# A one-core decoder layer in f32: the up stage of its experts in two passes, with the weights as the stationary operand

## The chip, the cores and the metric

The kernel runs on one core of a Trainium2 chip. The metric is the device time of one execution in microseconds; shown are the median of three executions and one profiled execution.

## What is computed

One decoder layer on 256 tokens of width 2048: a combined input projection, two kinds of attention, gates, an output projection, a layer norm, then a retrieval over 128 x 128 = 16384 single-neuron experts, and a last layer norm. The change sits in the last two:

```python
def peer(x, w_query, sub_keys_1, sub_keys_2, expert_down, expert_up):
    ...
        u = expert_down[et]
        h = jax.nn.gelu(jnp.einsum('cd,ced->ce', xt, u), approximate=False)
        vv = expert_up[et]
        return jnp.einsum('ce,ced->cd', gt * h, vv)
...
        y_p = peer(h, peer_w_query[l], ...)
        h = layer_norm(ALPHA * h + y_p, ln2_g[l], ln2_b[l])
```

Each token picks 128 experts (8 heads, 16 each) with gates. The kernel does it densely: it multiplies all experts' down rows with the tokens, takes gelu, multiplies by a gate matrix g that is zero except at the picks, and multiplies with all up rows. Only the last 16 tokens (`ROUTED`) are left out of the dense down product (`DENSE` = 240): their picked down rows are gathered.

## The kernel before

**Weights.** All weights come as a stream of 425 tiles of 128 x 2048 f32, each in two halves of 128 x 1024 (512 KB). SP loads a half into `raw` (four slots, refilled as soon as `lo_ready` says that DVE is done with it). For full precision each half is split: ACT copies it to an fp32r high part (`hi`, L461), DVE subtracts to get the low part (`lo`, L779). PE then makes three products: high x high, high x low, low x high. Two tiles are in work at a time: ACT and DVE make tile n+1 while PE uses tile n, and a half's slot is free when PE has used it (`half_used`).

**Down stage** (`down`, 128 tiles). For each 128 experts the weights are stationary (128 x 128) and the tokens move. High and low parts of the tokens lie side by side, 480 columns, so that one pass with the high weight makes two products (L1552, L1556), and one of 240 columns with the low weight the third (L1553, L1555). ACT and DVE add the two parts and take gelu; the result `act4` goes to `a_dram` in HBM, four tiles at a time, written by ACT's queue. Beside it DVE selects the top experts, and POOL scatters the gates into `g_dram` by indirect DMAs (L396), gathers the down rows of the 16 routed tokens (L403), and adds their results into g by 16 more indirect DMAs (`put_pair`, L413).

**Up stage** (`up`, L1577, 128 tiles of 128 experts x 2048 outputs). Here the multiplied activations m = a x g are stationary (128 experts x 128 tokens, high and low part) and the weights move, 256 columns at a time: two token halves, two weight halves, three products, four chunks, 48 matmuls a tile. All 8 banks of PSUM hold the sum. POOL loads a and g for four tiles at a time (`loads`, L381 and L382, two buffers); DVE multiplies (`m_mult`, L1199), ACT makes the high part (`m_high`, L687), DVE the low (`m_low`, L1204). The last two tiles are done bank by bank with 512 columns (`up_bank`, L1587 to L1589), so that the norm can begin.

**Last norm.** Tokens are on partitions. For each of two token halves: residual from `h1_n` (h1 in token order, made by 32 transposes at L1538 and 8 copies at L683 ahead of the down stage), sum by accumulators, squares on ACT, times `ln2_g`, plus `ln2_b`, and stores of 256 KB by SP.

**What sets the order.** Nothing is scheduled: each engine runs its own program in the order written, with semaphores between them. A wait holds everything behind it on its engine.

Of the kernel before, what the change touches and what calls it, by code (L numbers as in the profile page):

```python
# [80 lines left out]
PAIR_AT = [134, 139, 144, 149, 155, 160, 165, 170]  # L81
# [17 lines left out]
N_SMALL = 4 * KD + 2 * KL + 8  # L99
# [44 lines left out]
def build(nc, stream, x_t, const_in, small_in, keys_t, ln2, rows_dram, y_out, a_dram, g_dram):  # L144
# [5 lines left out]
    def sem(name):  # L150
# [12 lines left out]
    sb("gap_a", [P, 96])  # L163
    a_all = sb("a_all", [P, KD, 2 * T], F32R)
# [25 lines left out]
    h1_n = sb("h1_n", [P, TT, D], F32, peer_mem)  # L190
    ln2_s = sb("ln2_s", [P, 2, D], F32, peer_mem)
# [11 lines left out]
    query_mem.close()  # L203
    sc = sb("sc", [P, TT, 2 * PEER_HEADS, NKEYS], F32, down_mem)
    act4 = sb("act4", [P, 2, 4, T], F32, down_mem)
    work = sb("work", [P, TOPK * TOPK], F32, down_mem)
    cand = sb("cand", [P, TOPK * TOPK], F32, down_mem)
    pick = sb("pick", [P, 2, TOPK, TOPK], F32, down_mem)
    val = sb("val", [P, 3, TOPK], F32, down_mem)
    idx = sb("idx", [P, 3, TOPK], U32, down_mem)  # L210
    idx2 = sb("idx2", [P, 2, TOPK], U32, down_mem)
    idx_f = sb("idx_f", [P, 4, TOPK], F32, down_mem)
    slot = sb("slot", [P, 2, TOPK], F32, down_mem)
    lists = sb("lists", [P, TT, 3, GROUPS, COLUMNS], U32, down_mem)
    routed = sb("routed", [P, 3, COLUMNS], U32, down_mem)
    h_rows = sb("h_rows", [P, D], F32, down_mem)
    part = sb("part", [P, 2, DENSE], F32, down_mem)
    u_b = sb("u_b", [P, COLUMNS], F32, down_mem)
    val_b = sb("val_b", [P, COLUMNS], F32, down_mem)
    down_mem.close()  # L220
    up_mem = ExitStack()

    a_in = sb("a_in", [P, 2, 4, T], F32, up_mem)
    g_in = sb("g_in", [P, 2, 4, T], F32, up_mem)
    m_f = sb("m_f", [P, 2, T], F32, up_mem)
    sb("gap_m", [P, 96], F32, up_mem)
    m_hi = sb("m_hi", [P, 2, T], F32R, up_mem)
    m_lo = sb("m_lo", [P, 2, T], F32R, up_mem)
    y_s = sb("y_s", [P, TT, D], F32, up_mem)
    u_s = sb("u_s", [P, TT, D], F32, up_mem)  # L230
    sums = sb("sums", [P, TT, 4], F32, up_mem)
    squares_s = sb("squares_s", [P, TT, 4], F32, up_mem)
    moment = sb("moment", [P, TT, 4], F32, up_mem)
    junk = sb("junk", [P, 4, 512], F32, up_mem)
    up_mem.close()
# [13 lines left out]
    x_in, par_in, keys_in, ln2_in = [sem(f"x_in{q}") for q in range(4)], sem("par_in"), sem("keys_in"), sem("ln2_in")  # L249
# [20 lines left out]
    ones_ready, rows_in, routed_in, row_in = sem("ones_ready"), sem("rows_in"), sem("routed_in"), [sem(f"row_in{b}") for b in range(ROW_BUFS)]  # L270
    part_ready, gelu_done = sem("part_ready"), sem("gelu_done")
    dot_ready, ub_gelu, vb_ready, b_put = sem("dot_ready"), sem("ub_gelu"), sem("vb_ready"), sem("b_put")
    ag_in = [sem("ag_in0"), sem("ag_in1")]
    m_ready, mhi_ready, mlo_ready, y_ready = sem("m_ready"), sem("mhi_ready"), sem("mlo_ready"), sem("y_ready")
    nmean_ready, sd_ready, out_ready, y_done = (
        sem("nmean_ready"), sem("sd_ready"), sem("out_ready"), sem("y_done"))
    dve_step, act_step = sem("dve_step"), sem("act_step")

    a_flat = a_all.rearrange("p k t -> p (k t)")
    up_hi = a_flat[:, 16:16 + 2 * HALF].rearrange("p (s n) -> p s n", s=2)  # L280
    up_lo = a_flat[:, KD * T + 16:KD * T + 16 + 2 * HALF].rearrange("p (s n) -> p s n", s=2)

    def weights(t, hf, moved=False):

        return (up_hi[:, t.par, :], up_lo[:, t.par, :]) if moved and hf else (w_hi[t.slot(hf)], w_lo[t.slot(hf)])

    row_buf = [m.rearrange("p k t -> p (k t)")[:, D * b:D * b + D] for m in (qp, res) for b in range(2)]
# [5 lines left out]
    r_sq = h1_n.rearrange("p t (q n) -> p (t q) n", q=2)  # L293
# [32 lines left out]
    def _(sp):  # L326
# [20 lines left out]
        for tt in range(TT):  # L347
            for c in range(4):
                o = slice(512 * c, 512 * c + 512)
                sp.wait_ge(out_ready, 4 * tt + c + 1)  # L350
                sp.dma_start(y_out[tt][:, o], u_s[:, tt, o]).then_inc(y_done, 16)
        sp.wait_ge(y_done, 16 * 4 * TT)
# [3 lines left out]
    def _(pool):  # L356
# [20 lines left out]
        pool.wait_ge(h1_lo, KD)  # L377
        pool.dma_start(ln2_s[:], ln2.partition_broadcast(P)).then_inc(ln2_in, 16)
# [5 lines left out]
        pool.wait_ge(ht_ready, 8)  # L384
        for j in range(GROUPS):
            pool.dma_start(h_rows[ROUTED * j:ROUTED * j + ROUTED, :], h1_n[ROUTED_AT:P, 1, :]).then_inc(rows_in, 16)
# [1307 lines left out]
```

## Time and profile before

| | us |
|---|---|
| median of 3 executions (2403.88 to 2408.3) | 2405.1 |
| the profiled execution's own time | 2408.02 |
| its span (first to last instruction) | 2406.3 |
| PE busy in the span | 2387.1 |
| up stage's matmuls in the chain (L1577) | 685.75 |

The profile is of one execution; its time stands 2.9 us above the median and 1.7 above its span. PE is busy for nearly all of the span, but a busy engine may still be slowed or replaced, and the time that counts is the chain that ended last.

### The profile page before, as it was taken

The numbers are of one execution on the slowest core, as the hardware profiler recorded it, in microseconds if no ns is written. First come the engines' busy times: TensorE is split into PE (matmuls) and PEld (weight loads), VectorE is DVE, ScalarE is ACT, GpSimd is POOL, SyncE is SP. The second block draws the span as 40 slices with busy tenths as digits, with TensorE's granted clock in tenths as the row PEclk, the third lists the DMA queues.
The fourth block names the chain that finished last, engine by engine and source line by source line (L and its number), as shares of the span: only waits on it lengthen the run. The fifth ranks groups of instructions, "written<-read, shape, count | busy, mean of one in ns | idle before, by whom it ended". The sixth has DMA issues, their size and how long they took to land.

```text
span 2406.3 us, 50917 instructions
## 1 busy us (share of the span) xinstructions
PE 2387.1 (99%) x18832; PEld 2318.2 (96%) x18832; DVE 1568.7 (65%) x2620; ACT 1198.8 (50%) x1787; POOL 592.3 (25%) x428
## 2 busy tenths in 40 slices
PE   9999999999999999999999999999999999999997
PEld 9999999999999999999999999999999999999997
DVE  5555555646666666888888887755555555555556
ACT  5444444545554444666565655444444444444444
POOL 0000000000000000477668886786000000000000
PEclk9999999999999999999999999999999999999999
DMA  7666676554445665588888889988776677777764
GB/s 275 220 216 222 216 224 207 187 192 158 162 152 175 195 197 185 189 229 223 229 257 258 261 273 288 287 232 256 250 239 237 244 244 244 233 241 244 247 232 148
DMA packets 182974, 539.26 MB, mean 224 GB/s; under 512 B 53680, under 2 KB 53680, under 8 KB 180480
## 3 DMA queue, kind: packets, MB, share of 16 engines
q1 hardware_dynamic: 124128, 449.89, 56.0%
q0 software_dynamic: 54176, 71.81, 12.1%
q10 hardware_dynamic: 4608, 16.78, 2.3%
q8 instruction: 32, 0.52, 0.1%
q14 instruction: 30, 0.25, 0.0%
HBM read 501.55 MB, written 35.78 MB: 223 GB/s over the span
## 4 chain that ended last, share of the span: by engine, by line
PE 97%; DVE 2%; ACT 1%; DMA 0%; issue 0%; ACTq 0%; SPq 0%; DVEq 0%
PE ps L1301 37%; PE ps L1577 28%; PE ps L1556 9%; PE ps L1552 9%; PE ps L1555 5%; PE ps L1553 5%; PE ps L1340 1%; PE ps L1355 1%; PE ps L1342 0%; PE ps L1348 0%; PE ps L1370 0%; DVE w_first L779 0%; PE ps L1530 0%; PE ps L1356 0%; PE ps L1335 0%; ACT w_first L461 0%
## 5 line engine op out<-in xcount | busy, mean ns | idle before, releaser
L779 DVE TENSOR_TENSOR w_first<-raw,w_first 128x1024 fp32r<-128x1024 f32 x425 | 520.6, 1225 | 379.7 <-ACT w_first L461 379.3
L396 POOL DMA_INDIRECT g_dram<-lists x256 | 438.8, 1714 | 99.2 <-issue 81.5
L461 ACT ACTIVATE w_first<-raw 128x1024 fp32r<-128x1024 f32 x425 | 447.2, 1052 | 4.0 <-DMA raw<-stream 3.1
L779 DVE TENSOR_TENSOR w_second<-raw,w_second 128x1024 fp32r<-128x1024 f32 x299 | 366.0, 1224 | 3.2 <-ACT w_second L461 3.0
L461 ACT ACTIVATE w_second<-raw 128x1024 fp32r<-128x1024 f32 x299 | 314.2, 1051 | 4.7 <-DMA raw<-stream 4.3
L1301 PE MATMUL ps<-a_all,w_first 128*128 128x256 f32 x2472 | 307.7, 280 | 0.0
L1301 PE MATMUL ps<-a_all,w_second 128*128 128x256 f32 x2472 | 300.2, 277 | 0.2 <-DVE a_all L810 0.2
L1301 PEld LDWEIGHTS ps<-a_all,w_first 128*128 128x128 f32 x2472 | 292.3, 188 | 1.0
L1301 PEld LDWEIGHTS ps<-a_all,w_second 128*128 128x128 f32 x2472 | 290.4, 188 | 0.4 <-DVE a_all L810 0.4
L1577 PE MATMUL ps<-w_first,m_hi 128*128 128x256 f32 x2016 | 269.6, 276 | 0.0
L1577 PE MATMUL ps<-a_all,m_hi 128*128 128x256 f32 x1984 | 265.2, 276 | 0.0
L779 DVE TENSOR_TENSOR a_all<-raw,a_all 128x1024 fp32r<-128x1024 f32 x126 | 154.4, 1225 | 150.4 <-ACT a_all L461 150.4
L1577 PEld LDWEIGHTS ps<-w_first,m_hi 128*128 128x128 f32 x2016 | 247.3, 188 | 0.1
L1577 PEld LDWEIGHTS ps<-a_all,m_hi 128*128 128x128 f32 x1984 | 243.2, 188 | 0.0
L461 ACT ACTIVATE a_all<-raw 128x1024 fp32r<-128x1024 f32 x126 | 133.8, 1062 | 170.7 <-PE ps L1577 170.7
L1556 PE MATMUL ps<-a_all,w_second 128*128 128x480 f32 x512 | 193.9, 379 | 0.0
L1552 PE MATMUL ps<-a_all,w_first 128*128 128x480 f32 x512 | 193.8, 379 | 0.0
L1556 PE MATMUL ps<-a_all,w_first 128*128 128x480 f32 x512 | 193.7, 378 | 0.0
L1552 PE MATMUL ps<-a_all,w_second 128*128 128x480 f32 x512 | 193.6, 378 | 0.0
L692 ACT ACTIVATE part<-ps 128x240 f32<-128x240 f32 x128 | 47.6, 372 | 285.6 <-PE ps L1556 285.6
L381 POOL DMA_DIRECT2D a_in<-a_dram x32 | 17.1, 534 | 632.7 <-DVE m_f L1199 630.6
L687 ACT ACTIVATE m_hi<-m_f 128x256 fp32r<-128x256 f32 x128 | 53.3, 417 | 206.6 <-DVE m_f L1199 206.6
(245 smaller groups left out, 4399.0 us busy)
## 6 DMA issues: line engine op xcount, KB each, us to landing
raw<-stream SPq DMA_DIRECT2D x850, 512.0 KB, 3.4
g_dram<-rot POOLq DMA_DIRECT2D x32, 512.0 KB, 6.1
a_dram<-act ACTq DMA_DIRECT2D x32, 512.0 KB, 3.7
a_in<-a_dram POOLq DMA_DIRECT2D x32, 512.0 KB, 5.1
g_in<-g_dram POOLq DMA_DIRECT2D x32, 512.0 KB, 6.4
g_dram<-lists POOLq DMA_INDIRECT x256
res<-x_t SPq DMA_DIRECT2D x4, 512.0 KB, 7.4
ln_s<-ln POOLq DMA_DIRECT2D x1, 2048.0 KB, 8.3
```

Of the source, the lines that this page charges most:

```text
L396: pool.indirect_dma_start(out=g_cell, out_offset=bass.IndirectOffsetOnAxis(ap=lists[0:n, tt, 1, j, c:c + 1], axis=0), in_=lists[0:n, tt, 2 ...
L461: act.activation(weights(t, hf, moved)[0], raw[:, t.slot(hf), :], ACT.Copy).then_inc(hi_ready, 1)
L687: act.activation(m_hi[:, par, :], m_f[:, par, :], ACT.Copy).then_inc(mhi_ready, 1)
L692: act.activation(part[:, t.par, :], acc[t.par][:, DENSE:2 * DENSE], ACT.Copy).then_inc(part_ready, 1)
L779: dve.tensor_tensor(low, raw[:, s, :], high.bitcast(F32), ALU.subtract).then_inc(lo_ready, 1)
L1301: ins = pe.matmul(out, w, a, start=first and q == 0, stop=last and q == 2)
L1340: ins = pe.matmul(ps_s[:, o:o + k1], q_s[:, q0:q0 + P], k_s[:, 0:k1], start=True, stop=not rope)
L1552: pe.matmul(both, wh, a_all[:, kk, 0:2 * DENSE], start=kk == 0, stop=False)
L1553: ins = pe.matmul(high, wl, a_all[:, kk, 0:DENSE], start=False, stop=False)
L1555: pe.matmul(high, wl, a_all[:, kk, 0:DENSE], start=False, stop=False)
L1556: ins = pe.matmul(both, wh, a_all[:, kk, 0:2 * DENSE], start=False, stop=kk == KD - 1)
L1577: ins = pe.matmul(ps[:, o:o + 256], m[:, b % 2, s], w[:, 256 * c:256 * c + 256], start=first and q == 0 and c % 2 == 0, stop=False, skip_g ...
```

## The change

**Up stage.** It now has the form of the down stage: the weights are stationary, 128 x 128, and m moves, its high and low parts side by side in `m_two` (480 columns, high weight), then 240 columns with the low weight. Outputs lie on partitions: one bank of PSUM for 128 outputs, 8 banks for 1024. So the experts are gone through twice, pass 0 for outputs 0 to 1023 and pass 1 for the rest, 64 tiles each; a tile's two halves are now two blocks of 128 experts x 1024 outputs. The stream has the same number of halves. PE makes 32 matmuls a tile.

**m in pass 1.** A block of four (512 experts, 32 of them, `BLOCKS`) is multiplied by g once in pass 0 (`m_mult`, one instruction of 960 columns, at every second tile) and stays in SBUF where there is room: 21 slots (`SLOTS_M`). The first 6 results of gelu never go to HBM (`KEPT`). Blocks 19 to 31 share two slots in pass 0, so that POOL's `load` of block u, from 21 on, waits for `mlo_ready` of block u-2. Pass 1 begins with the last two blocks, then the 19 resident ones, and loads and multiplies the last 11 again.

**Routed tokens.** g is no longer changed for them (`put_pair` is gone). Their up rows are gathered by 16 indirect DMAs of 128 rows (`x_fetch`), DVE scales and adds them (`x_add`, at every third tile of pass 1 from tile 70 on), and 16 small matmuls sum over each token's eight groups (`x_sums`, between tiles 119 and 120).

**Between the passes.** The last tile of pass 0 is done bank by bank (`by_bank`); ACT copies the low part (`low_s`), DVE adds the high part to the residual, and the first tile of pass 1 goes bank by bank too.

**Last norm.** Features are on partitions. The residual times ALPHA minus its mean is made early (`hsum`, one matmul, `scale_res`). At the end the sum over features and squares is made by matmuls with ones; DVE centres and scales 16 x 256 columns, ACT applies gain and bias, and SP stores `y_out` as features x tokens. 16 transposes and 4 copies ahead of the down stage go, as does the load of `ln2`.

```diff
+KEPT, SLOTS_M = 6, 21
+RESIDENT = SLOTS_M - 2
+USES = list(range(BLOCKS)) + [BLOCKS - 2, BLOCKS - 1] + list(range(BLOCKS - 2))
...
+MULT_USES = list(range(BLOCKS)) + list(range(BLOCKS + SLOTS_M, 2 * BLOCKS))
+MULT_AT = [2 * u - 2 for u in range(BLOCKS)] + [2 * (BLOCKS + 8 + 2 * j) for j in range(BLOCKS - SLOTS_M)]
+X_AT = [2 * (BLOCKS + 3) + 3 * c for c in range(COLUMNS)]
...
-        def loads(i, b):
-            pool.dma_start(a_in[:, b], a_dram[i * 2 + b]).then_inc(ag_in[b], 16)
-            pool.dma_start(g_in[:, b], g_view[i * 2 + b]).then_inc(ag_in[b], 16)
...
+        def load(k):
+
+            u, b = MULT_USES[k], k % 2
+            if k >= 2:
+                pool.wait_ge(m_ready, k - 1)
...
+            earlier = [v for v in range(u) if USE_SLOT[v] == USE_SLOT[u]]
+            if earlier:
+                pool.wait_ge(mlo_ready, 2 * earlier[-1] + 2)
+            pool.dma_start(g_in[:, b], g_view[USES[u]][:, :, 0:DENSE]).then_inc(ag_in[b], 16)
+            if USES[u] >= KEPT:
+                pool.dma_start(m_slot[USE_SLOT[u]], a_dram[USES[u]]).then_inc(ag_in[b], 16)
...
+        for q in range(2 * PASS):
+            if q in MULT_AT:
+                m_mult(MULT_AT.index(q))
+            if q + 1 < 2 * PASS:
+                lo(Tile(T_UP + q + 1))
+                m_low(q + 1)
+            if 4 <= q < 8:
+                scale_res(q - 4)
...
+            if q in X_AT:
+                x_add(X_AT.index(q))
...
+        def wide(t, hf, m, c, start=False):
+            return pe.matmul(bank[c][:, 0:2 * DENSE], w_hi[t.slot(hf)][:, P * c:P * c + P], m_two[:, m, 0:2 * DENSE],
+                             start=start, stop=False, skip_group_check=True)
+
+        def narrow(t, hf, m, c):
+            return pe.matmul(bank[c][:, 0:DENSE], w_lo[t.slot(hf)][:, P * c:P * c + P], m_two[:, m, 0:DENSE],
+                             start=False, stop=False, skip_group_check=True)
...
+        for k in range(KD):
+            act.wait_ge(w_ready, k // 4 + 1 if k < 12 else 4 + (k - 12) // 2)
+            act.activation(res[:, k, :], res[:, k, :], ACT.Identity, scale=small[:, S_G2 + k:S_G2 + k + 1],
+                           bias=small[:, S_B2 + k:S_B2 + k + 1]).then_inc(out_ready, 1)
```

The order of instructions at the places of which the prediction speaks. First PE in the steady part of the up stage, the first half of a tile before (the program's name for the second half's weights is `a_all`, whose memory they use) ...

```order
L1577 MATMUL ps<-w_first,m_hi 128x256 [waits lo_ready,mlo_ready]
L1577 MATMUL ps<-w_first,m_hi 128x256 x7
L1577 MATMUL ps<-w_first,m_lo 128x256 x4
L1577 MATMUL ps<-w_first,m_hi 128x256 x8
L1577 MATMUL ps<-w_first,m_lo 128x256 x4
```

... and of the change, where a half has 8 matmuls of 480 columns and 8 of 240:

```order
L1622 MATMUL ps<-m_two,w_first 128x480 [waits lo_ready,mlo_ready]
L1626 MATMUL ps<-m_two,w_first 128x240 x2
L1622 MATMUL ps<-m_two,w_first 128x480 x2
L1626 MATMUL ps<-m_two,w_first 128x240 x2
L1622 MATMUL ps<-m_two,w_first 128x480 x2
L1626 MATMUL ps<-m_two,w_first 128x240 x2
L1622 MATMUL ps<-m_two,w_first 128x480 x2
L1626 MATMUL ps<-m_two,w_first 128x240 x2
L1622 MATMUL ps<-m_two,w_first 128x480
```

So 24 matmuls became 16, and the operands changed places. Next DVE in pass 0, late blocks (`more` is the memory of the two shared slots, `sc` that of the gates just loaded):

```order
L1246 TENSOR_TENSOR m_two<-more,m_two 128x2x240 [waits mhi_ready]
L1240 TENSOR_TENSOR more<-more,sc 128x960 [waits ag_in1]
L809 TENSOR_TENSOR w_first<-raw,w_first 128x1024 [waits hi_ready]
L809 TENSOR_TENSOR w_second<-raw,w_second 128x1024 [waits hi_ready]
L1246 TENSOR_TENSOR m_two<-more,m_two 128x2x240 [waits mhi_ready]
L809 TENSOR_TENSOR w_first<-raw,w_first 128x1024 [waits hi_ready]
L809 TENSOR_TENSOR w_second<-raw,w_second 128x1024 [waits hi_ready]
L1246 TENSOR_TENSOR m_two<-more,m_two 128x2x240 [waits mhi_ready]
```

The multiplication L1240, which waits for a load, stands ahead of the next tile's two weight splits and its m_low. POOL at the same place:

```order
L409 DMA sc<-g_dram 128x4x240 [waits m_ready]
L411 DMA more<-a_dram 128x960
L409 DMA sc<-g_dram 128x4x240 [waits mlo_ready,m_ready]
L411 DMA more<-a_dram 128x960
```

From block 21 on each pair of loads waits for `mlo_ready`, an m_low of DVE, as well as for `m_ready`.

## Rows read from the trace of the kernel before

**Rows 1.** The page: the chain of work that ended last, by engine and by line.
```profile
PE 97%; DVE 2%; ACT 1%; DMA 0%; issue 0%; ACTq 0%; SPq 0%; DVEq 0%
PE ps L1301 37%; PE ps L1577 28%; PE ps L1556 9%; PE ps L1552 9%; PE ps L1555 5%; PE ps L1553 5%; PE ps L1340 1%; PE ps L1355 1%; PE ps L1342 0%; PE ps L1348 0%; PE ps L1370 0%; DVE w_first L779 0%; PE ps L1530 0%; PE ps L1356 0%; PE ps L1335 0%; ACT w_first L461 0%
```

**Rows 2.** Windows: stretch, length, busy of PE, PEld, DVE, ACT, POOL, clock, DMA share, GB/s.
```profile
1500.00:1600.00 100.00, 100.00 (x611) 91.49 (x611) 68.67 (x75) 49.11 (x78) 79.68 (x48) 1.00 0.91 268
1900.00:2000.00 100.00, 100.00 (x885) 100.00 (x884) 58.73 (x76) 45.46 (x56) 6.46 (x10) 1.00 0.71 242
2300.00:2406.00 106.00, 93.06 (x771) 90.54 (x769) 67.47 (x102) 46.49 (x71) 2.58 (x4) 0.96 0.55 189
```

**Rows 3.** Timeline, down stage, PE: start us, us, engine, line, tile, shape.
```profile
1023.43 0.46 PE L1552 MATMUL ps<-a_all,w_first 128*128 128x480 f32 x1
...
1686.11 0.38 PE L1552 MATMUL ps<-a_all,w_first 128*128 128x480 f32 x1
1686.32 0.27 PE L1553 MATMUL ps<-a_all,w_first 128*128 128x240 f32 x1
1686.76 0.38 PE L1552 MATMUL ps<-a_all,w_first 128*128 128x480 f32 x1
...
1695.95 1.15 PE L1577 MATMUL ps<-w_first,m_hi 128*128 128x256 f32 x8
```

**Rows 4.** Chain of waits in order of time, around the down stage and in the up stage.
```profile
1020.01 3.66 PE ps L1538 x32
1696.11 685.75 PE ps L1577 x6048
```

**Rows 5.** Timeline, ACT and DVE, where the up stage begins.
```profile
1698.83 1.05 ACT L461 ACTIVATE w_second<-raw 128x1024 fp32r<-128x1024 f32 x1
...
1696.55 0.41 DVE L1144 TENSOR_TENSOR part<-ps,part 128x240 f32<-128x240 f32 x1 [0.36 <-ACT part L692]
1700.11 1.22 DVE L779 TENSOR_TENSOR w_second<-raw,w_second 128x1024 fp32r<-128x1024 f32 x1
1701.24 1.22 DVE L779 TENSOR_TENSOR w_first<-raw,w_first 128x1024 fp32r<-128x1024 f32 x1
```

**Rows 6.** Timeline, mid up stage: one m_mult of 256 columns.
```profile
2035.97 0.42 DVE L1199 TENSOR_TENSOR m_f<-a_in,g_in 128x256 f32<-128x256 f32 x1
```

**Rows 7.** Landings of g_in, then POOL's issues and landings of a_in, 1700 to 2390 us.
```profile
DMA to landing us min/median/max: 5.7/6.3/7.2
L381 POOL DMA_DIRECT2D a_in<-a_dram x30: 528/531/536, 1710.8 to 2341.7; - x30
DMA to landing us min/median/max: 4.4/5.1/5.5
```

**Rows 8.** Landings of g_in, us, from 1600 to 1690 us.
```profile
DMA to landing us min/median/max: 7.1/8.7/10.2
```

**Rows 9.** Timeline: ACT's copies of token rows, and POOL's first DMA after them.
```profile
1020.85 4.07 ACT L683 ACTIVATE h_n<-ps 128x512 f32<-128x512 f32 x8
1025.21 3.88 POOL L386 DMA_DIRECT2D h_rows<-h_n  x8 [7.29 <-ACT h_n L683]
```

**Rows 10.** DMA queues, 1700 to 2390 us: packets, MB, share of 16 engines.
```profile
q1 hardware_dynamic: 36000, 131.09, 56.2%
q0 software_dynamic: 8640, 31.46, 13.9%
```

**Rows 11.** DVE and ACT pieces: line, operation, tile, shape, count, busy us, mean ns.
```profile
L1029 DVE RECIPROCAL n_rstd<-n_rstd 128x256 f32<-128x256 f32 x1 | 1.7, 1745 | 0.0
L1144 DVE TENSOR_TENSOR part<-ps,part 128x240 f32<-128x240 f32 x128 | 52.1, 407 | 89.1 <-ACT part L692 87.2
...
969.30 1.30 ACT L652 ACTIVATE qp<-qp,gain 128x256 f32<-128x256 f32 x3
```

**Rows 12.** Timeline: last matmul, last DVE work; the span ends at 2406.3.
```profile
2392.66 0.40 PE L1589 MATMUL ps<-a_all,m_lo 128*128 128x512 f32 x1
2400.37 2.74 DVE L1264 SCALAR_TENSOR_TENSOR u_s<-u_s,moment,ln_s 128x512 f32<-128x512 f32 x4
```

More of the change, by code:

```diff
@@ L1206, in _ @@
         add_low(NKEYS - 2)
         lo(Tile(T_UP))
[L1208 to L1211 removed]
+        m_mult(0)
+        m_low(0)
         add_low(NKEYS - 1)
[L1214 to L1229 removed]
@@ L1557, in down @@
                 ins.then_inc(half_used, 1)
-        with pe.Fori(0, NKEYS // 8) as i:
+        with pe.Fori(0, NKEYS // 8 - 1) as i:
             for b in range(8):
                 down(Tile(T_DN + b, i, 8))
-        def up(t, n, b, moved=True, first=False):
-            pe.wait_ge(mlo_ready, n + 1)
+        pe.wait_ge(hsum_ready, 2)
+        pe.matmul(ps_s[:, 0:T], ones, hsum, start=True, stop=True).then_inc(hsum_mm, 1)
+        for b in range(8):
+            down(Tile(T_DN + NKEYS - 8 + b))
@@ L1579, in up @@
[L1579 to L1589 removed]
+                m = 2 * (b % 2) + hf
@@ new lines, in up @@
+                start = first and hf == 0
+                for c in (1, 3, 4, 5, 6, 7, 0, 2) if start else range(8):
+                    if start and c == 4:
+                        pe.wait_ge(shift_ready, 1)
+                    if start and c in (0, 2):
+                        u = next(u for u in (Tile(T_UP - 2), Tile(T_UP - 1)) if u.par == c // 2)
+                        pe.wait_ge(acc_free[u.par], u.pair + 2)
+                    if x_first and hf == 0:
+                        pe.wait_ge(x_out, c + 1)
+                    if c % 2 == 0 or start:
+                        wide(t, hf, m, c, start)
+                        ins = narrow(t, hf, m, c)
+                    else:
+                        narrow(t, hf, m, c)
+                        ins = wide(t, hf, m, c)
@@ L1591, in _, with x_sums @@
+        def x_sums():
+            pe.wait_ge(x_ready, COLUMNS)
+            for c in range(8):
+                for k, o in ((c, 480), (c + 8, 496)):
+                    ins = pe.matmul(bank[c][:, o:o + ROUTED], x_acc[:, P * k:P * k + P], small[:, S_SEL:S_SEL + ROUTED],
+                                    start=False, stop=False, skip_group_check=True)
+                ins.then_inc(x_mm, 1)
         for b in range(8):
-            up(Tile(T_UP + b), b, b, b > 1, b == 0)
-        with pe.Fori(1, NKEYS // 8 - 1) as i:
+            up(Tile(T_UP + b), b, b, b == 0)
@@ new lines, in _ @@
+        last = ((t, 1, 1), (u, 0, 2), (u, 1, 3))
+        for c in range(8):
+            for of in last:
+                wide(*of, c)
+                ins = narrow(*of, c)
+            ins.then_inc(y_ready, 1)
+        pe.wait_ge(zs_ready, 5)
+        pe.matmul(bank[0][:, 0:T], ones, zsum_s, start=True, stop=False)
+        for c in range(4, 8):
+            pe.wait_ge(z_ready, c + 1)
+            ins = pe.matmul(bank[0][:, 0:T], ones, res[:, 8 + c, :], start=False, stop=c == 7)
+        ins.then_inc(zsum_mm, 1)
@@ L1611, in build @@
+        pe.wait_ge(half_sums, 1)
+        pe.matmul(bank[1][:, 0:T], ones, sqsum_s, start=True, stop=False)
+        for c in range(8):
+            pe.wait_ge(zsq_ready, c + 1)
+            ins = pe.matmul(bank[1][:, 0:T], ones, sq_s[:, c, :], start=False, stop=c == 7)
+        ins.then_inc(zsq_mm, 1)
     ctx.close()
```

520 lines of the change are left out of this document (280 added, 240 removed).

## The prediction

> **What bounds the kernel now.** I read the page's chain first: PE holds 97% of it, 28% of the span in the up stage's L1577 [rows 1]. So what counts is how long PE needs for its work and where it would have to wait. The windows come next: in both late stages PE is busy for all of each 100 us at clock 1.00, that is 2.4 GHz, while DVE is at 59 to 69 and the DMA engines at 0.71 to 0.91 of theirs [rows 2]. Last comes the timeline, for start-to-start times, since a matmul's own duration overlaps the next. In the down stage the four matmuls of two weight blocks (480, 240, 240, 480 columns) take 1686.76 - 1686.11 = 0.65 us; the whole stage of 128 tiles takes 1695.95 - 1023.43 = 672.5 us, 5.25 a tile [rows 3]. In the up stage 6048 matmuls of 256 columns take 685.75 us, 113.4 ns each, 5.44 a tile [rows 4].
>
> **The sum, part by part.**
>
> 1. *Matmuls of the up stage.* Now 697.1 us, from 1695.95 [rows 3] to the end of the last matmul, 2392.66 + 0.40 = 2393.06 [rows 12]. The change gives each tile the down stage's 32 matmuls with the same operands' shapes and order, so I take that stage's 672.5 whole: **-24.6**. The change removes a third of the matmuls but only 6% of the columns (11520 for 12288 a tile). TensorE: Matmul & The Clock Gate, "Back-to-back issue gap", in the Trainium skill, gives a gap of N/2.4 + 2.5 ns in warm state. An estimate by that page alone: 109 ns for 256 columns, 305 for a pair of 480 and 240, so -46 instead of -24.6. The rows show 113.4 and 5.25 us / 16 = 328, and the rows decide.
>
> 2. *Ahead of the down stage.* 32 transposes take 3.66 us [rows 4], and 16 of them go: -1.8. Their copies on ACT are halved too, so they hide nothing new. The added `hsum` matmul costs under 0.3: **-1.6** together. Its two DVE reductions, as well as the removed `put_pair`, the `ln2` load and the six stores, lie beside a PE that waits for none of them.
>
> 3. *First tiles of the up stage.* At tile 0 DVE is done with `add_low` at 1696.96; ACT's two splits for tile 1 end at 1699.88, DVE's second at 1701.33 [rows 5]. New behind it is m_low(1), 480 columns. DVE needs 1.14 us from start to start for 1024 columns (1701.24 - 1700.11) and 0.42 for 256 [rows 6], so about 0.6: ready at 1701.9, when a tile of 5.25 is over at 1701.2. **+0.8** with the wakeup. The multiplication of block 1 fits in ahead, before 1698.96. Bound below: 0, if ACT runs earlier; above: 2, if block 1's gates are late.
>
> 4. *The shared slots of pass 0.* This is the new wait. For blocks 21 to 31 POOL may issue the loads only after m_low of block u-2's second half, and DVE multiplies at the head of the tile, with two weight splits and m_low behind it. The cycle is: wakeup of POOL 0.3 (ACT ends at 1024.92, POOL issues at 1025.21) [rows 9]; the two loads, which before took 0.53 + 6.3 = 6.8 from first issue to last landing [rows 7]; multiplication of 960 columns 1.1, two splits 2.3, m_low 0.6, so 4.0. Together 11.1 us, where two tiles are 10.5. Each of 11 blocks thus slips by 0.6. At first m_low ends 3.1 us into a tile (ACT's second split may start when the tile starts, 1.1; DVE's split to 2.4; m_low to 3.1), so 2.1 of slack is used up first: 11 x 0.6 - 2.1 = **+4.5**. Bounds: the loads at 6.3, the longer one alone, give 10.6 and nothing after the slack; the 8.7 that a g_in took beside the scatters [rows 8], plus 0.5, gives 13.5 and 11 x 3 - 2 = 31. I take the unloaded row, since POOL has nothing else in flight here. DMA: Bandwidth & Descriptors, "Anatomy of one DMA", in the Trainium skill fits a GpSimd DMA with 2.0 us plus bytes over 436 GB/s. An estimate by it: 3.1 us for 0.49 MB, about 5 for the pair, and no stall. The landings of 5.1 and 6.3 beside the stream are longer, so the rows stand.
>
> 5. *DMA traffic.* The stream moves 1.05 MB in 5.25 us: 200 GB/s. Queue 1 moved 131.09 MB in 0.562 of 690 us, so the engines would carry 338 GB/s; queue 0 by the same division 328 [rows 10]. Pass 0 adds 0.98 MB per two tiles, 94 GB/s: share 0.59 + 0.29 = 0.88. Tiles 70 to 115 of pass 1 add 16 gathers of 1.05 MB and 11 pairs of loads: 27.6 MB in 241 us, 114 GB/s: share 0.94. PE stood still at no time with 0.91 [rows 2], so I cost it at **0**; above see the rivals.
>
> 6. *Between the passes, x, DVE.* In tile 63 DVE begins its eight additions at 3.1 us (0.4 each [rows 11]) and ends about 1 us after the tile, when PE needs bank 7 only 4.6 us into the next; tile 65's m_low is ready at 9.8 of 10.5: **0**, at most +2. The 16 matmuls of `x_sums` cost the 0.114 of a transpose each: **+1.8**. An `x_add` of 2048 columns takes DVE 2.3 us every third tile; with a multiplication in the next tile m_low ends at about 4.0 of 5.25: covered. Were the cover gone, each would cost its overrun, under 1 us.
>
> 7. *The end.* Before, the span ends 13.2 us after the last matmul (2406.3 - 2393.06) [rows 12]. Now, from that point: DVE adds low and high part of a bank (0.45 + 0.34), for four banks also the running sum (0.34 + 0.11), against 0.98 of PE a bank, and is behind by 0.5 at bank 7, so it is done at +1.4. Sum by matmul, mean: +2.5. Then DVE alone: centre 1024 columns 1.15, variance 0.4, centre 1.15, reciprocal of 256 columns 1.75 [rows 11], five more passes of 1024 at 1.15, two waits on itself, two passes of 512 at 0.6: +14.0. ACT is behind: after the last full pass at +12.8 it has 8 pieces of 0.42 left (three took 1.30 [rows 11]): +16.2. From the last DVE work, 2403.11, the last store took 3.2 [rows 12]: +19.4. So **+6.1**, uncertain by 3.
>
> Sum: -24.6 - 1.6 + 0.8 + 4.5 + 0 + 1.8 + 6.1 = **-13.0** against the profiled span of 2406.3. The profiled execution took 2408.0, 2.9 above the median of 2405.1; I carry the difference to the median: 2392.
>
> **The rivals.**
>
> A. *The slots cost nothing.* The loads are done within 6.3, or the wakeup is quicker. For: the landings are counted from the issue, and the two overlap. Against: 0.53 + 6.3. Result 2392 - 4.5 = 2387.5, by the same sum.
>
> B. *The slots bind hard.* Place: L1240 in DVE's program in tiles 40 to 60. Price: 11 x (cycle - 10.5) - 2.1. Break-even with before is at 17.5 us of stall, a cycle of 12.3, so loads of 8.0 from first issue to last landing; at 9.2 the result is 2392 + 26 = 2418. For: the landings of 7.1 to 10.2 under load [rows 8], and 0.88 of the engines in use. Against: no landing after 1700 us took more than 7.2 [rows 7].
>
> C. *DMA becomes the bound in pass 1.* 75.8 MB in 46 tiles. If the engines carry only 268 / 0.91 = 295 GB/s [rows 2], that is 257 us for 241: +16, result 2408. Against: that window's bytes were scattered in single words, these are rows of 8 KB and 1 KB.
>
> D. *Fewer matmuls count more than columns.* By the page's gap the change would be worth 21 us more. As a mechanism here: the new stage would run a pair faster than the down stage's 328 ns, since each matmul goes to another bank. Then 2371. Against: before, L1301 stays in one bank and L1577 changes it, both near 113 ns.
>
> E. *The clock falls.* The clock stood at 1.00 in the up stage, in which PE changes banks all the time, and at 0.96 in the last window, which holds PE's end [rows 2]. In the new up stage it would fall only if the waits of part 4 were long. If a tenth of the stage went at 1.2 GHz, that is +67. TensorE: Matmul & The Clock Gate, "psum-queue depth-cycling", in the Trainium skill reports a clock that oscillates when a kernel cycles through PSUM banks. The trace does not show that here, where 256-column matmuls do cycle.
>
> F. *The edit is made but eaten*: several edges (parts 3, 6, 7) each at their upper bound, +2, +2, +3, with 4 more in the slots: 2400 to 2403.
>
> **How the numbers follow.** Forecast (2389 to 2396) 0.59; A 0.14; B 0.08 (half of it above 2410, half within 2400 to 2410); C 0.06; D 0.03; E 0.01; F 0.09. A measurement here can tell 0.2%, 4.8 us, so faster means below 2400.3, slower above 2409.9. Faster: 0.59 + 0.14 + 0.03 and half of F, with a little of B: 0.82. Same: half of F, half of C, part of B: 0.10. Slower: the rest, 0.08. The range of 8 in 10 holds the forecast and A, and of F and B what lies below 2402: 2385 to 2402.
>
> **What would show each step.** Part 1: 0.65 us for four matmuls at L1622 and L1626, 5.25 a tile; 5.44 or under 5.0 makes it wrong. Part 2: the down stage begins 1.8 us earlier. Part 4: idle time of PE before the matmuls of every second tile from 41 on, DVE's L1240 waiting for g or a by 1 to 3 us, in 11 places; no idle is A, more than 1.5 us a block is B. Part 5: share 0.88 and 0.94, and ACT never waiting long for `raw`; waits for it in tiles 70 to 115 are C. Part 7: 19 us from the last of the up stage's matmuls to the end, with one reciprocal of 1.75 and PE's sums in its first 2.5. The prediction is wrong if the up stage with all its waits is not 677 to 683 us from its first matmul to its last.

## The result and the profile after

| | before | after |
|---|---|---|
| median, us | 2404.8 (2403.9 to 2408.3, 5 executions) | 2422.4 (2419.8 to 2428.7, 5 executions) |
| profiled execution: its time, span | 2408.0, 2406.3 | 2422.2, 2420.4 |

The ratio after to before is 1.0075, 95% interval 1.0063 to 1.0086: slower by 0.75%, where 0.5% faster was forecast. In the third set of runs below (e9 to e12, on one chip) it was 1.0073 (1.0058 to 1.0089). Executions of the kernel before fall on separate levels, 2404 to 2405, 2408, 2430 and 2435 to 2437 us, and beside e1 to e4 10 of 13 stood at 2430, which makes the ratios of that set too good by nearly 1%. The experiments are therefore compared with the changed kernel's 2422.4, and with before's 2404.8. The changed kernel ran again only beside e11 and e12, and had 2426.7 there; a difference of some 4 us between sets says nothing.

First the chain that ended last, on the page (it answers to [rows 1]).

```profile
PE 90%; DVE 4%; DMA 4%; ACT 1%; issue 0%; POOL 0%; ACTq 0%; POOLq 0%
```

PE has lost 7 points of it, to DVE and to DMA. The list of waits names the edge:

```profile
DVE more L1240 <- DMA more<-a_dram: 64.9, 11, 7.6
```

The columns are total us, times, longest: eleven waits, one for each of blocks 21 to 31. The windows (columns as in [rows 2], here PE alone: busy, count, clock, DMA share, GB/s) say when PE suffers from it:

```profile
1700.00:1800.00 100.00, 100.00 (x611) 1.00 0.82 293
1900.00:1950.00 50.00, 45.23 (x272) 1.00 0.69 248
1950.00:2000.00 50.00, 40.60 (x228) 0.93 0.61 216
2000.00:2050.00 50.00, 42.83 (x257) 1.00 0.75 282
2050.00:2100.00 50.00, 50.00 (x306) 1.00 0.72 261
2150.00:2250.00 100.00, 100.00 (x610) 1.00 0.84 318
```

Outside of 1900 to 2050 the stage keeps 611 matmuls in 100 us. Inside it makes 272 + 228 + 257 = 757 where 918 had room. In the middle window the clock is at 0.93 of 2.4 GHz besides: 178 ns for each matmul (40.60 / 228), in place of 164. The DMA share of these windows, 0.61 to 0.75, is a mean over 50 us and hides what happens within a turn. One turn, from the chain of waits in order of time (start, us, what):

```profile
1930.73 0.58 DVE m_two L1246
...
1931.35 0.49 issue
1931.84 0.74 POOL sc L409
1932.58 7.67 DMA more<-a_dram
...
1940.27 1.16 DVE more L1240
1941.43 1.14 DVE w_first L809
1942.57 1.13 DVE w_second L809
1943.70 0.58 DVE m_two L1246
```

m_low ends at 1931.31; POOL issues the gates 0.5 later, the activations 0.74 after them; they land 7.67 later; then the multiplication, two weight splits and the next m_low, 4.0. That is 13.0 us. From the start of the first of these multiplications, 1902.27, to that of the eleventh, 2034.76, it is 132.5 us for ten turns, 13.25 each, where PE needs a block every 10.5. The transfer took 6.16 us in the first of the eleven and 6.97 to 8.65 in the ten behind it:

```profile
1896.08 6.16 DMA more<-a_dram
...
2000.41 8.65 DMA more<-a_dram
```

The first was issued before anything had stalled. From the third on DVE, behind each wait, makes four weight splits in a row (1928.38 to 1933.57 in the turn above). Each frees a slot of `raw`, so SP issues four halves of the stream at 1929.76, 1930.89, 1932.60 and 1933.73, 2.1 MB, beside the 0.98 MB of the pair. Here are windows of this turn, while the pair is under way and behind it, and then two around PE's longest wait, 3.7 us ahead of 1958.88:

```profile
1931.84:1940.25 8.41, 8.41 (x53) 1.00 0.89 327
1940.25:1944.40 4.15, 1.98 (x12) 1.00 0.12 44
...
1954.00:1958.00 4.00, 1.20 (x8) 0.89 0.00 2
1958.00:1962.00 4.00, 3.12 (x10) 0.50 0.81 262
```

So the DMA engines are busy while the pair is under way and nearly or wholly idle while PE stands still. Behind that longest wait the clock is at its lower level, 1.2 GHz: ten matmuls take 3.12 us, some 310 ns each.

The end, PE and DVE in the timeline:

```profile
2398.42 0.27 PE L1626 MATMUL ps<-m_two,w_second 128*128 128x240 f32 x1
2398.53 0.60 PE L1718 MATMUL ps<-row_mem,cst 128*128 128x256 f32 x2
2398.97 1.89 PE L1721 MATMUL ps<-res,cst 128*128 128x256 f32 x8
...
2404.78 0.43 DVE L1330 SCALAR_TENSOR_TENSOR row_mem<-ps,row_mem 128x256 f32<-128x256 f32 x1 [2.20 <-PE ps L1727]
...
2406.26 1.75 DVE L1334 RECIPROCAL row_mem<-row_mem 128x256 f32<-128x256 f32 x1
```

A matmul of f32 operands appears as two: the four of L1721 are x8. The fourteen of the norm fill PE from 2398.7 to 2404.8, 0.43 us each, and DVE waits 2.2 us for the squares. From 2398.69 to the end it is 21.7 us. The sums of the routed tokens, ahead of tile 120, stand in one row:

```profile
2349.71 3.80 PE L1677 MATMUL ps<-small,h_rows 128*128 128x16 f32 x32
```

**Where the time went.** All against the profile of before. The down stage begins at 1017.78 for 1023.43, -5.65: some 1.8 of it are the transposes, the other 3.8 lie in code that is unchanged, and the profile in e9 puts them down to chance. Down stage: from 1017.78 to 1691.92, 674.1 for 672.5, +1.6, of which 0.94 is a wait of PE for the first m_low. Up stage to the end of its last matmul, 2398.69: 706.8 for 697.1, +9.7. End: 21.7 for 13.2, +8.5. The sum is +14.1, as the spans have it.

### The profile page after: what moved, and what is told of

The parts are those of the page before. It is cut to its first block, busy times and chain, and to the rows that moved or that the text cites. A ratio compares the mean times of both kernels' runs of the same rounds, so it can differ in the third digit from the quotient of the medians.

```text
span 2420.4 us, 46061 instructions
## 1 busy us (share of the span) xinstructions
PE 2374.9 (98%) x16878; PEld 2244.5 (93%) x16878; DVE 1644.8 (68%) x2569; ACT 1227.7 (51%) x1797; POOL 609.1 (25%) x443
## 3 DMA queue, kind: packets, MB, share of 16 engines
q0 software_dynamic: 53280, 92.27, 14.1%
## 4 chain that ended last, share of the span: by engine, by line
PE 90%; DVE 4%; DMA 4%; ACT 1%; issue 0%; POOL 0%; ACTq 0%; POOLq 0%
PE ps L1355 36%; PE ps L1622 15%; PE ps L1610 9%; PE ps L1606 9%; PE ps L1626 7%; PE ps L1609 5%; PE ps L1607 5%; DMA more<-a_dram 3%; DVE w_first L809 1%; PE ps L1394 1%; DVE w_second L809 1%; PE ps L1409 1%; DVE more L1240 1%; PE ps L1424 0%; PE ps L1396 0%
## 5 line engine op out<-in xcount | busy, mean ns | idle before, releaser
L809 DVE TENSOR_TENSOR w_second<-raw,w_second 128x1024 fp32r<-128x1024 f32 x425 | 520.2, 1224 | 104.4 <-ACT w_second L490 103.1
L490 ACT ACTIVATE w_second<-raw 128x1024 fp32r<-128x1024 f32 x425 | 447.8, 1054 | 191.0 <-PE ps L1622 178.2
L1622 PE MATMUL ps<-m_two,w_first 128*128 128x480 f32 x1024 | 332.3, 384 | 22.8 <-DVE m_two L1246 22.8
L1622 PE MATMUL ps<-m_two,w_second 128*128 128x480 f32 x1024 | 328.3, 380 | 0.5 <-DVE m_two L1246 0.5
L1626 PEld LDWEIGHTS ps<-m_two,w_first 128*128 128x128 f32 x1024 | 194.2, 190 | 28.4
L1626 PEld LDWEIGHTS ps<-m_two,w_second 128*128 128x128 f32 x1024 | 192.8, 188 | 28.8
L1626 PE MATMUL ps<-m_two,w_first 128*128 128x240 f32 x1024 | 201.9, 276 | 0.0
L1626 PE MATMUL ps<-m_two,w_second 128*128 128x240 f32 x1024 | 199.8, 274 | 0.0
L1622 PEld LDWEIGHTS ps<-m_two,w_first 128*128 128x128 f32 x1024 | 167.3, 192 | 27.6 <-DVE w_second L809 16.3
L1622 PEld LDWEIGHTS ps<-m_two,w_second 128*128 128x128 f32 x1024 | 165.2, 189 | 1.7 <-DVE w_second L809 0.7
```

The source lines that it names most:

```text
L490: act.activation(w_hi[t.slot(hf)], raw[:, t.slot(hf), :], ACT.Copy).then_inc(hi_ready, 1)
L809: dve.tensor_tensor(w_lo[s], raw[:, s, :], w_hi[s].bitcast(F32), ALU.subtract).then_inc(lo_ready, 1)
L1622: return pe.matmul(bank[c][:, 0:2 * DENSE], w_hi[t.slot(hf)][:, P * c:P * c + P], m_two[:, m, 0:2 * DENSE], start=start, stop=False, skip_ ...
L1626: return pe.matmul(bank[c][:, 0:DENSE], w_lo[t.slot(hf)][:, P * c:P * c + P], m_two[:, m, 0:DENSE], start=False, stop=False, skip_group_ch ...
```

## Experiments

Theory Q: the shared slots of pass 0 form a ring (m_low, POOL, two transfers, multiplication, splits, m_low) that is longer than two tiles, and what is worth 28 us is its length, an order of operations. Rival D: the bytes, whatever the order; rival X: the gathered rows.

**e1.** In DVE's program the multiplication goes behind the splits and m_low.

```diff
-            if q in MULT_AT:
-                m_mult(MULT_AT.index(q))
             if q + 1 < 2 * PASS:
                 lo(Tile(T_UP + q + 1))
                 m_low(q + 1)
+            if q in MULT_AT:
+                m_mult(MULT_AT.index(q))
```

> DVE's multiplication by the gates stands behind the next tile's two weight splits and m_low instead of ahead of them; the loads, slots and bytes are the same. Theory Q (the loss is the ring through the shared slots: m_low, POOL's loads, multiplication, splits, m_low, 13.25 us where two tiles are 10.5): the splits no longer stand in the ring, PE's waits in tiles 41 to 61 vanish, 25 us faster than the change, about 2397 us. Rival D (DMA bandwidth in pass 0: the loads and the stream slow each other, whatever the order): at most 5 us faster, PE still waits there.

Measured: 2394.8 us (2394.5 to 2396.5), 27.6 below the changed kernel. The same bytes move, and in less time, so rival D falls. DVE's waits for the activations:

```profile
  DMA more<-a_dram: 0.8, 1
```

PE makes 307, 307 and 306 matmuls in the three windows in which it made 757 in all.

**e2.** In `load` the gates are issued ahead of the wait for the slot, since they don't need it.

```diff
+            pool.dma_start(g_in[:, b], g_view[USES[u]][:, :, 0:DENSE]).then_inc(ag_in[b], 16)
             if earlier:
                 pool.wait_ge(mlo_ready, 2 * earlier[-1] + 2)
-            pool.dma_start(g_in[:, b], g_view[USES[u]][:, :, 0:DENSE]).then_inc(ag_in[b], 16)
```

> POOL issues the load of g before it waits for the slot, and only the load of a behind it. Theory Q: the ring loses the 0.74 us of g's issue and the second transfer in flight, 13.25 becomes 0.5 + 5 to 6.5 + 4.0 = 9.5 to 11, so 20 to 26 us faster than the change, 2396 to 2402 us. Rival D: the same bytes in the same stretch, at most 5 us faster.

Measured: 2394.6 us (2393.1 to 2398.7). The waits for activations are 4.2 us in 7 places, hidden from PE.

**e3.** Three shared slots and 18 resident blocks in place of 2 and 19.

```diff
-RESIDENT = SLOTS_M - 2
+SHARED = 3
+RESIDENT = SLOTS_M - SHARED
```

> Blocks 18 to 31 share three slots instead of blocks 19 to 31 two; still 21 slots, 11 loads again in pass 1. Theory Q: a load starts a block earlier and the ring may take 21 us, waits gone, 25 us faster than the change, about 2397 us. Rival D: at most 5 us faster.

Measured: 2397.2 us (2396.9 to 2398.6). It is 2.4 and 2.6 us above e1 and e2; its profile shows one more wait of PE, 0.71 us at 1708, and no other in pass 0. Three edits at three different places of the ring each take all but 2 or 3 of the 28 us; the transfers' sizes are the same in all of them.

**e4.** The gathered rows of the routed tokens are left out, with their additions and sums.

```diff
-        for _, e in sorted(late_loads + late_rows):
+        for _, e in sorted(late_loads):
...
-        x_sums()
```

> The routed tokens' up rows are left out (no gathers, no x_add, no x_sums, no x_out), so the outputs of the last 16 tokens lack their expert part; all else is the change. Theory Q: 3.7 us of x_sums and under 2 us around it, 2417 us, the waits of pass 0 stay. Rival X (the gathers make the second pass wait for DMA or DVE): 15 us or more faster than the change.

Measured: 2419.4 us (2415.5 to 2423.0), 3.0 less. The turns are still 13.2 us (1902.28 to 2034.26 in ten). What went is about the 3.8 us that `x_sums` holds PE. X falls. On D this run says nothing, since it leaves the bytes of pass 0 as they are.

**e5.** Which part of the turn is long, and why? For blocks 21 to 31 only the activations are loaded.

```diff
-            pool.dma_start(g_in[:, b], g_view[USES[u]][:, :, 0:DENSE]).then_inc(ag_in[b], 16)
+            if not BARE[0] <= k < BARE[1]:
+                pool.dma_start(g_in[:, b], g_view[USES[u]][:, :, 0:DENSE]).then_inc(ag_in[b], 16)
```

> The changed kernel, with the gates' transfer left out for blocks 21 to 31 of pass 0 (those blocks are multiplied by gates that are already there), everything else in place. It asks what makes a turn of the ring 13.2 us long. Theory S (the two transfers of a turn share the engines with the stream, and the activations, issued second, land late because of the gates ahead of them): alone, the activations land in 5 to 6 us, as in the kernel that issues the gates first (median 5.4), the turn is 0.5 + 5.5 + 4.0 = 10.0 us, under 10.5, and the waits go: 2394 to 2398 us, PE idle in tiles 41 to 61 under 3 us. Rival L (the landing of one transfer beside the stream takes 7 to 8.6 us whatever is ahead of it): the turn is still 12 to 13 us, 15 to 25 us of idle PE stay, 2410 to 2420 us.

Measured: 2395.4 us (2393.3 to 2399.4). The landings of one line's transfers from 1895 to 2006 us, first L411 of the changed kernel (behind the gates), then the same load in e5 (alone):

```profile
L411 POOL DMA_DIRECT2D more<-a_dram x9: 549/549/552, 1896.1 to 2000.4; - x9
...
DMA to landing us min/median/max: 6.2/7.9/8.7
```
```profile
L413 POOL DMA_DIRECT2D more<-a_dram x11: 537/539/552, 1895.2 to 2000.9; - x11
...
DMA to landing us min/median/max: 4.4/4.9/6.6
```

The waits are gone, as theory S said: PE has none between 1700 and 2350. But the 3.0 us between 7.9 and 4.9 are not the price of the gates ahead, since e5 took away the gates and the stall together. In e1 and e3 the pair is issued as in the changed kernel, gates first, activations 0.74 behind them, and nothing stalls. The same rows of e1, then of e3:

```profile
L411 POOL DMA_DIRECT2D more<-a_dram x11: 549/552/552, 1895.5 to 2000.6; - x11
...
DMA to landing us min/median/max: 5.3/6.1/6.9
```
```profile
L412 POOL DMA_DIRECT2D more<-a_dram x10: 549/552/552, 1896.9 to 1991.7; - x10
...
DMA to landing us min/median/max: 5.3/5.5/6.0
```

So the gates ahead cost 0.75 us of issue and 0.6 to 1.2 of landing. The other 1.8 to 2.4 come with the stall. In e3 the stream's halves are issued one by one, 2.3 to 2.8 us apart, and the windows while a pair is under way and behind it are these:

```profile
1938.27:1944.47 6.20, 6.20 (x40) 1.00 0.91 312
1944.47:1948.80 4.33, 4.33 (x28) 1.00 0.70 265
```

The changed kernel's turn had 0.89 and 0.12 there. The engines are as full in both while the pair is under way, but 2.75 MB pass until it has landed (8.41 us at 327 GB/s) in place of 1.93. That the bunched halves are what slows the pair is read from these rows; no run delays them alone. In e2, where the gates follow the activations, the activations land in 5.5 and the gates in 7.1, and nobody waits for the gates there. (DMA: Bandwidth & Descriptors, "Anatomy of one DMA", in the Trainium skill would give an estimate of 3.1 us for such a transfer; beside the weight stream the rows have 4.9 alone.)

**e8.** e1 and e2 together, on a second chip with the three that follow.

> The changed kernel with both reorderings at once: the gates issued ahead of the wait, and the multiplication behind the weight splits and m_low. If the ring was the only thing that stood in the way (theory Q), each edit alone has already taken all of it, and both together give what one gives, 2393 to 2396 us, with no wait of DVE for activations. If something of the ring was left in each (rival R), it is 2 to 5 us below them, 2389 to 2392.

Measured: 2394.1 us (2392.8 to 2396.7), no wait for activations; what either gives. Q holds against R.

**e6.** e2, with the first multiplication ahead of the down stage's last additions, and the two sums over eight chunks in halves.

```diff
+        m_mult(0)
         add_low(NKEYS - 2)
         lo(Tile(T_UP))
-        m_mult(0)
         m_low(0)
...
-                dve.tensor_reduce(zsum_s, res[:, 0:8, :].rearrange("p k t -> p t k"), AX_X, ALU.add).then_inc(zs_ready, 1)
+                link(dve.tensor_tensor(sq_s[:, 0:4, :], res[:, 0:4, :], res[:, 4:8, :], ALU.add))
```

> The kernel with the gates issued first, and two edits at the edges: the first multiplication of the up stage stands ahead of the last additions of the down stage, and the two sums over eight chunks (3.9 us each, strided) become additions in halves of 4, 2 and 1 chunks, spread over two tiles each. Theory: the waits of PE at those places go, 0.94 at the first tile, 0.57 and 0.45 behind the sums, so 2.0 us: profiled span 2389.3 for 2391.3. Rival: the 0.94 is hidden by the weight splits of tile 0 anyway, or the additions in halves delay m_low as much as the sums did; then the span stays at 2391.

Measured: 2393.7 us (2391.7 to 2397.3, 12 executions). The profiled span, 2392.1, is no better than e2's. The waits of PE in the up stage, by the timeline, are these:

```profile
1696.35 0.49 PE L1630 MATMUL ps<-m_two,w_first 128*128 128x480 f32 x1 [0.55 <-DVE m_two L1248]
1707.46 0.49 PE L1630 MATMUL ps<-m_two,w_first 128*128 128x480 f32 x1 [0.33 <-DVE m_two L1248]
2362.20 0.45 PE L1630 MATMUL ps<-m_two,w_second 128*128 128x480 f32 x1 [0.47 <-DVE m_two L1248]
```

So of the three waits two are gone (0.94 and 0.57), and two have come: tile 0 now starts 1.1 earlier, and tile 1 waits 0.55 for its m_low. The third was no matter of the sums: it stands ahead of the last two tiles, for which PE wants both m_low at once. The balance is 0.6 us, and PE's pace differs by more between the two profiles (609 matmuls in 100 us here, 611 in e2: 2 us over the stage). The theory gave 2.0 and was wrong in more than half of it.

**e7.** e6, and the squares summed by fp32r matmuls.

```diff
-            ins = pe.matmul(bank[1][:, 0:T], ones, sq_s[:, c, :], start=False, stop=c == 7)
+            ins = pe.matmul(bank[1][:, 0:T], ones_r, sq_r[:, 8 + c, :], start=False, stop=c == 7)
```

> The same as e6_starts, and the sum of squares at the end by matmuls with ones in fp32r (one matmul of about 0.12 us) in place of f32 (0.45 us each, issued as two). It leaves out precision in that sum alone. Theory: the nine products take 1.1 instead of 4.1 us, the last of them then waits for the last square on ACT (ready about 2.0 us behind the last matmul of the up stage), and DVE, which waited 2.2 us for them, waits for nothing: 2.0 to 2.6 us less, span 2387. Rival: DVE's own chain of mean, centring and variance takes the place of the wait, and the gain is under 1 us.

Measured: 2393.0 us (2391.3 to 2395.5), span 2390.3 (2387 was expected, 2 of it from e6), ratio to before on that chip 0.9927 (0.9900 to 0.9954). The end, from 2370.87, is 19.4 us, 2.3 less than the 21.7 of e6, as expected:

```profile
2372.68 0.47 PE L1737 MATMUL ps<-sq_r 128*128 128x256 f32 x1
2372.98 1.11 PE L1740 MATMUL ps<-sq_r 128*128 128x256 f32 x8
```

Eight matmuls in 1.1 us, for sixteen in 3.5. DVE's 2.2 us of waiting are gone. This is the lowest median of all.

**e10, e11.** The changed kernel again, and the ring made longer by useless DVE work inside each of its eleven turns, on a third chip.

```diff
+            if RESIDENT + 2 <= k < BLOCKS:
+                for _ in range(2):
+                    link(dve.tensor_tensor(gap_l ...
```

> The changed kernel, unchanged, on the chip of the next run, as its base and for a second profile: 2418 to 2426 us, a turn of the ring 13.0 to 13.5 us, waits of DVE for the activations 60 to 70 us in 11 places.

> The changed kernel with two additions of 480 columns on DVE, to memory that nothing reads, behind the multiplication of each of blocks 21 to 31 of pass 0: some 1.2 us more DVE work inside each turn of the ring, 11 times, which elsewhere would be hidden in DVE's idle time. Theory Q (the turn is serial: wakeup, transfers, multiplication, splits, m_low, and its length sets the time): each turn grows by 1.1 to 1.3 us, the kernel by 11 to 14 us, 2433 to 2437. Rival T (the transfers set the pace, and DVE's work beside them has slack): under 3 us more, 2422 to 2426. If the turns grow by less than the added work, part of the landing time was contention that a longer turn relieves.

Measured: e10 2426.7 us (2422.9 to 2431.6), just above what was expected; its profile is of the slowest execution, its turns in the profile were 13.8 us, not 13.0 to 13.5 (1902.10 to 2039.87 in ten), and its waits 69.4. e11: 2440.8 us (2438.7 to 2444.0), 14.1 more. The added work takes 1.3 us a turn:

```profile
1961.99 1.16 DVE L1240 TENSOR_TENSOR more<-more,sc 128x960 f32<-128x960 f32 x1 [7.78 <-DMA more<-a_dram]
1963.07 1.34 DVE L1243 TENSOR_TENSOR gap_l<-small 128x480 f32<-128x480 f32 x2
```

Turns of 15.06 us (1901.36 to 2051.95) against 13.78: +1.28, and 11 x 1.28 = 14.1. The medians are of four executions each, on two levels, and agree with this better than they need to: the two profiled spans differ by 12.4 (2442.2 and 2429.8), the two lowest times by 15.9. Either is far from rival T's 3. DVE is idle for 7.8 us in that turn, and 1.3 us more of its work still costs 1.3: the place in the turn counts, not the load of the engine. The activations land in 8.2 us (median) where e10 has 8.5, so a longer turn hardly relieves them.

**e12.** e7, with the centring of the last four chunks on POOL.

```diff
+        for k in range(12, 16):
+            pool.tensor_tensor(res[:, k, :], res[:, k, :], mean_s, ALU.add).then_inc(pool_centred, 1)
...
-        link(center(12, 4))
```

> The same as e7_ends, and the centring of the last four chunks on POOL (four additions of 256 columns, 1.73 us each by POOL's rows at the start, so 7 us, from the mean on) in place of one of DVE's passes of 1.14 us. Theory: POOL is done 2 us before DVE needs it, and the tail falls by 1.1 us, to 18.3 from the last matmul of the up stage to the end. Rival: the two engines hinder each other, DVE's passes become longer by as much or more, and the tail stays at 19.4 or grows.

Measured: 2393.2 us (2391.1 to 2393.9), the same as e7. POOL was quicker than expected (4.78 us for the four). Beside it DVE's passes of 1024 columns took up to 1.42 us instead of 1.21, and DVE was done 0.8 us earlier, counted from the last matmul of the up stage. Yet the end stays at 19.4 us (2372.57 to 2392.0), and the reason is neither theory's. First ACT in e7, then in e12:

```profile
2383.84 4.04 ACT L799 ACTIVATE res<-res,small 128x256 f32<-128x256 f32 x8 [0.32 <-DVE res L1335]
```
```profile
2383.58 6.00 ACT L804 ACTIVATE res<-res,small 128x256 f32<-128x256 f32 x12 [0.32 <-DVE res L1340]
```

ACT's pieces, 0.5 us each, now queue behind DVE twelve long instead of eight, and end 17.0 us after the last matmul in both.

**e9.** The kernel before, once more.

> The kernel before, unchanged, for a second profile of it. In the profile of it that was read, the stages ahead of the down stage take 1023.4 us, and in all five profiles of the changed kind 1017.1 to 1017.8, of which only the 1.8 of the removed transposes is due to the change. Theory K (the kernel's own layout decides it): the new profile shows 1023 again, with tiles of 5.66 us in the first 400 us. Rival N (chance of one execution or chip): it shows 1019 to 1020, with tiles of 5.46. If its time is near 2430, where most executions of it on one chip were, the profile should show where those 25 us lie: theory, spread over all stages in proportion to matmuls; rival, in one place.

Measured: 2430.2 us for the profiled execution, median 2408.1 over ten, four of them between 2404.5 and 2405 and two at 2430.2. Its windows, the same columns as [rows 2], and then a row of the first profile:

```profile
200.00:400.00 200.00, 200.00 (x1730) 199.10 (x1730) 107.40 (x164) 90.93 (x144) 13.42 (x19) 1.00 0.70 222
1900.00:2000.00 100.00, 100.00 (x851) 100.00 (x850) 56.69 (x71) 42.84 (x53) 5.17 (x8) 1.00 0.68 227
```
```profile
200.00:400.00 200.00, 200.00 (x1713) 199.16 (x1712) 107.16 (x170) 91.85 (x145) 13.41 (x19) 1.00 0.67 217
```

Theory K falls: the same code begins the down stage at 1018.97 here, as rival N said, so the 1023.43 of the first profile was chance. The span is 22.2 us longer all the same, and what is longer lies in one place, as the second rival said: the up stage's 6048 matmuls, in the chain,

```profile
1691.65 712.38 PE ps L1577 x6048
```

take 712.4 us for the 685.75 of [rows 4], 26.6 more, 117.8 ns each for 113.4, with the clock at 1.00 and no wait in either. Less the 4.5 at the start that is the 22.2.

## Why the prediction was wrong

The forecast failed at part 4, its one new wait. Rival B, given 0.08 (half of it above 2410), is what happened, at the place and in the tiles that it named. Point by point:

- **Part 1, the matmuls (-24.6): right.** Four matmuls in 0.65 us, 306 in 50 us, 5.25 us a tile, wherever nothing waits. Rival D did not come true: the gap that TensorE: Matmul & The Clock Gate, "Back-to-back issue gap", in the Trainium skill gives, 305 ns for a pair as an estimate, is not that of this stage either, which has 328. (That section gives the formula for an isolated matmul.)
- **Part 2 (-1.6): right.** The down stage begins 1.67 us (1016.11 to 1017.78) behind the first of the 16 transposes that are left. **Part 3 (+0.8):** it was hidden by another wait that was missed, 0.94 ahead of the first up tile, because m_mult(0) stood behind the last split. In e6, where that one is gone, tile 1 waits 0.55.
- **Part 4 (+4.5; measured 26 to 29): wrong.** 28.8 is the up stage of the changed kernel, 706.8, less that of e2, 678.0 (1691.52 to 2369.52). Between 1915 and 2040 alone PE makes 603 matmuls where e2 makes 762, 26.1 us at 164 ns. The ring, the formula and the slack were right: 11 x (13.25 - 10.5) - 2.1 = 28.2. The step that failed is one term and the reason for it: "the two loads, which before took 0.53 + 6.3 = 6.8", taken as a fixed price "since POOL has nothing else in flight here". In the mean of ten turns they took 0.74 + 7.8 = 8.6, besides 0.5 for the wakeup (once 1.6) in place of 0.3. For a ring that has not stalled yet the term was right: 0.74 + 6.16 = 6.9 in the first turn, 0.74 + 6.1 in e1. With it a turn is 0.5 + 6.9 + 4.0 = 11.4 and the same formula gives 7.8 us. The other 20 are what the forecast left out: once a turn is longer than two tiles, the waits bunch the stream's own loads around the pair, the landing grows by up to 2.5 us, and the turn with it (the growth is measured, the bunch as its cause is read from the rows beside e5). The row came from a stage with time in its buffers, whose loads met no such bunch. The bound of 31, from the 8.7 of [rows 8], lay near the result, but those landings stood beside the scatters; that it fits is in part luck. The forecast's own break-even, a cycle of 12.3 us, lies only 1.2 above its 11.1, and a chance of 0.08 for that was too little.
- **A cost missing in the sum:** the clock. Between 1915 and 2040 PE waits 21.4 us; the other 4.7 of the 26.1 are slower matmuls, most of them behind the longest wait, where the clock was at 0.50. Rival E had named long waits as the condition, but priced it only for a tenth of the stage.
- **Part 5 (0): right as a mean, not within a turn.** Shares are 0.82 and 0.84 over 100 us, and PE does not stall at 318 GB/s. The forecast's 0.88 and 0.94 were too high, since the engines carried more than 338 GB/s: 318 / 0.84 = 379. But "PE stood still at no time with 0.91" was no reason for a cost of nothing: a share does not say how long one transfer takes. While a pair is under way it is 0.91 in e3 and 0.89 in the changed kernel, with landings of 5.5 and 7.7 us, and the price is in part 4.
- **Part 6:** `x_sums` took 3.8 us, not 1.8, since its 16 matmuls are f32 and are issued as 32. A term was missed: the first of the two sums over eight strided chunks takes DVE 3.9 us and makes PE wait 0.57, and ahead of the last two tiles PE waits 0.45, which has nothing to do with the sums (e6).
- **Part 7 (19.4; measured 21.7):** "Sum by matmul, mean: +2.5" left out that nine f32 products for the squares follow at 0.43 each. DVE's part was right, with the reciprocal at 1.75.
- **In code that nobody touched:** -3.8 us, chance in the profile of before; in e9 the same code is 4.5 us faster.

With the ring mended, and its smaller errors put in as measured, the forecast's sum closes; this is bookkeeping behind the result, no second forecast. Without the 4.5 of the slots its span would be 2388.8; add 2.0 for `x_sums`, 1.0 for the two waits of part 6, 2.3 for the end, 0.8 (1.6 in place of 0.8) for the first tile and its surroundings, and take off 3.8: 2391.1. The span of e2 is 2391.3.

## What to carry to other kernels

Where a change lets a buffer be refilled only after its last reader, write down the whole turn, from the last read through the wakeup, the transfers in their order of issue, and every instruction that stands ahead of the next last read, and compare it with the time for which the consumer is content. If it is longer, or near enough that a small error makes it so, it can decide the result, and a busy share of the DMA engines averaged over many turns does not show it: here 11.4 us for 10.5 became 13.25. The price of a transfer is not fixed. Once the consumer stalls, the other streams refill in bunches, and the transfer that is waited for lands among them; so work the turn out a second time with the landing that such a bunch would give. The remedies are free here: move out of the turn what need not be in it (the gates' load, the multiplication ahead of the splits), or let a load begin a block earlier with one more shared slot.

## What the runs showed of the chip

- Two transfers of 480 KB issued 0.75 us apart land after 5.1 and 6.1 us (e1; 4.9 and 5.5 in e3) beside a stream whose loads of 512 KB are issued one by one, mostly 2.5 to 2.8 us apart, and after 6.6 and 7.9 (changed kernel) where four of those loads are issued within 4 us around the pair; one alone lands after 4.9 (e5). All are medians from 1895 to 2006 us.
- The same program runs the same matmul stream at one of two paces, by execution: 113.4 or 117.8 ns per matmul of 256 columns in the up stage of before (26.6 us over the stage), and 1713 or 1730 matmuls in 200 us in an earlier stage (some 4 us). Fast and slow in the two stages would give four sums, 2404, 2408, 2430 and 2435, and these are the levels on which its executions fell. Only two profiles show it, so how a level is chosen stays open. The new form of the stage, with 480 and 240 columns, showed no second pace of that size: where the ring does not stall it takes 678 to 682 us in eight profiles.
- Small f32 matmuls cost by their number: 32 of 16 columns took 3.8 us, and one f32 product of 256 columns 0.43 us, where eight in fp32r took 1.1 in all (e7).
- With all eight banks in turn the clock stayed at 1.00. What TensorE: Matmul & The Clock Gate, "psum-queue depth-cycling", in the Trainium skill reports was not seen. In the changed kernel's pass 0 the clock fell behind the longest wait of PE, 3.7 us, and not behind the others, up to 3.1. In e1, e3 and e7 it was also 0.97 from 2300 to 2350 us, the stretch that holds `x_sums`; in e2 and e6 it was 1.00 there.
